# Sliding-window attention: value products and spreads issued two units at a time, their outputs copied and scaled once per pair

## The chip, the cores and the metric

One core of one Trainium2 chip runs the whole program. The metric is the device time of one execution in microseconds (us), and the lower it is the better. The engines are TensorE (PE in the rows, its weight loads PEld), VectorE (DVE), ScalarE (ACT), GpSimd (POOL) and SyncE (SP, which here only issues DMAs). Each engine takes its own instructions in order, and semaphores join them.

## The reference, cut to what matters

The reference is two blocks of two layers on 512 tokens of width 1024. The change touches one stage of it, the sliding-window attention of the second block, and nothing else:

```
q = q.reshape(B, nb, BLOCK, N_KV_HEADS, Q_PER_KV, HEAD_DIM)
...
scores = einsum("bnqgrd,bnkgd->bngrqk", q, kb) * (HEAD_DIM ** -0.5)
scores = scores - slopes * dist, masked outside the window
m = maximum(max(scores), sink)
p = exp(scores - m)
probs = p / (sum(p) + exp(sink - m))
out = einsum("bngrqk,bnkgd->bnqgrd", probs, vb)
return out.reshape(B, S, Q_DIM) @ w_o + b_o
```

There are 16 query heads in 4 groups (one key and value head each) and 4 blocks of 128 tokens. A block attends to itself and to the block before it; the first block has only itself.

## The kernel before, in words

The stage is worked in 16 **units**, u = 0 to 15. Unit u is key head g = u // 4 and token block n = u % 4, with the four query heads of that group. A unit with n = 0 has one block of keys instead of two, so about half the work in transposes and products.

What each unit needs, and who does it:

- **Scores** (TensorE, `swa_scores`, L1092): 12 matmuls into PSUM banks 0 and 1 for even units, 2 and 3 for odd ones.
- **Largest score** (VectorE, `swa_max`, L2357): the sink column is written (L2364), then four fused instructions add the distance term and take the minimum of the negated scores (L2366).
- **Exponentials** (ScalarE, `swa_exp`, L1700): four activations with their row sums (L1707). VectorE inverts the sums (`swa_inverse`, L2376).
- **Transposes** (TensorE, `swa_transposes`, L1111; recorded at the helper's line L643): four into bank 4 for the previous block of keys, if there is one, then four into bank 5 for the unit's own block. Banks 4 and 5 exist once each, so the transposes of unit u wait until both halves of the unit before were copied out (L1115 and L1117).
- **Copies** of the transposed probabilities (`spt`, two buffers): ScalarE copies bank 4 (`swa_copy`, L1713), VectorE copies bank 5 (`swa_copy`, L2370, the row at L2374).
- **Products** with the values (TensorE, `swa_pv`, L1122; rows at L1132): eight matmuls, four if n = 0, into one half of bank 6.
- **Spread** of the inverted sums over the partitions (TensorE, `swa_spread`, L1138; rows at L1146): eight matmuls into one half of bank 7.
- **Output**: ScalarE copies the unit's half of bank 6 to `so` (`swa_out`, L1719), and VectorE multiplies it with the half of bank 7 (`swa_scaled`, L2381, row at L2386).

ScalarE's plain copies all have the line L1318. After each group of four units `so` is split in two parts: ScalarE's `swa_hi` (L1726) and VectorE's `swa_low` (L2389, row at L2392), which wait for the group's scalings. In units 10 to 13 VectorE also splits a quarter each of the first weight panel of the output projection (`split_piece`, L1855, rows at L1860 and L1861).

The order on each engine is written out by hand:

```
PE:  scores(0) scores(1); for u: scores(u+2), transposes(u), pv(u-1), spread(u-1);
     then spread(15), pv(15), output projection
ACT: exp(0); for u: exp(u+1), copy(u) if u % 4, out(u-1), at u = 5, 9, 13 hi
DVE: max(0), values of four token blocks, max(1); for u: inverse(u), max(u+2), copy(u),
     scaled(u-1), at u = 6, 10, 14 low, at u = 10 to 13 split_piece
```

The output projection (`out_projection`, L866) follows on TensorE. Its first panel is taken one tile of the contraction at a time, 6 matmuls each, and tile i waits for the i-th `swa_low` (semaphore "mixed"). Weight panels come by DMA from SyncE.

Of the kernel before, what the change touches and what calls it, by code (L numbers as in the profile page):

```python
# [34 lines left out]
P = 128  # L35
D = 1024
KT = D // P
TX, TC = 512, 256
# [52 lines left out]
def build_kernel(nc, dram, out):  # L91
    with ExitStack() as ctx:
# [44 lines left out]
        ps = ctx.enter_context(nc.psum_tensor("ps", [P, 8, 512], F32))  # L137
# [64 lines left out]
        so, sqh = place("so", 25600, [8, TX]), parts("sqh", 25600, [8, TX])  # L202
# [214 lines left out]
        def _(pe):  # L417
# [291 lines left out]
            for e in range(2, 16):  # L709
                if 4 <= e < 12:  # L710
                    side, j = ROPE[e - 4]
# [225 lines left out]
            for t in range(2):  # L937
                for f in range(4):
                    for c in range(2):
                        at = f % 2 * 256 + c * P  # L940
# [181 lines left out]
            def swa_pv(u):  # L1122
                g, n = u // 4, u % 4
                pe.wait_ge(sa["copied"], WITH_PREV[u + 1])
                pe.wait_ge(sa["copied_dve"], u + 1)
                if u:
                    pe.wait_ge(sa["out"], u)
                if u == 1:
                    pe.wait_ge(sa["v_prev"], 2)
                for kt in range(0 if n else 1, 2):  # L1130
                    for half in range(2):
                        last = pe.matmul(ps[64 * half:64 * half + 64, 6, u % 2 * 256:u % 2 * 256 + 256],  # L1132
                                         (sv if kt else svp)[:, n - 1 + kt, g * 64:g * 64 + 64],
                                         spt[u % 2][:, kt, half * 256:half * 256 + 256],
                                         start=kt == (0 if n else 1), stop=kt == 1)
                last.then_inc(sa["pv"], 1)

            def swa_spread(u):  # L1138
                pe.wait_ge(sa["inverse"], u + 1)
                if u:  # L1140
                    pe.wait_ge(sa["scaled"], u)
                for j in range(2):
                    for half in range(2):
                        at = 32 + 4 * (u % 4) + 2 * half + j
                        to = u % 2 * 256 + j * P
                        last = pe.matmul(ps[64 * half:64 * half + 64, 7, to:to + P],  # L1146
                                         stat[:, at:at + 1].broadcast_to([P, 64]), ident, start=True, stop=True)
                last.then_inc(sa["spread"], 1)
# [3 lines left out]
            for u in range(16):  # L1152
                if u + 2 < 16:
                    swa_scores(u + 2)
                if u == 0:
                    pe.wait_ge(v_free, 4)
                swa_transposes(u)
                if u:
                    swa_pv(u - 1)
                    swa_spread(u - 1)  # L1160
            swa_spread(15)
            swa_pv(15)
            out_projection("wo", "mixpost0", h2hi, h2lo, sa["mixed"])
# [138 lines left out]
        def _(act):  # L1302
# [14 lines left out]
            def copy(o, in_, func=ACT.Identity, **kw):  # L1317
                return act.activation(o, in_, func, **kw)  # L1318
# [231 lines left out]
            for k in range(4):  # L1550
                n, s = FIRST["out0"] + k, k % 2
# [164 lines left out]
                    act.wait_ge(sa["pv"], u - 1)  # L1716
                copy(spt[u % 2][:, 0, :], ps[:, 4, :]).then_inc(sa["copied"], 1)

            def swa_out(u):  # L1719

                g, n = u // 4, u % 4
                act.wait_ge(sa["pv"], u + 1)
                copy(so[:, 2 * g:2 * g + 2, n * P:(n + 1) * P],
                     ps[:, 6, u % 2 * 256:u % 2 * 256 + 256].rearrange("p (j n) -> p j n", j=2)).then_inc(sa["out"], 1)

            def swa_hi(g):  # L1726
                act.wait_ge(sa["scaled"], 4 * (g + 1))
                for t in range(2 * g, 2 * g + 2):
                    copy(h2hi[:, t, :], so[:, t, :]).then_inc(sa["mixed_hi"], 1)

            swa_exp(0)
            for u in range(16):
                if u + 1 < 16:
                    swa_exp(u + 1)
                if u % 4:
                    swa_copy(u)
                if u:
                    swa_out(u - 1)
                if u % 4 == 1 and u > 4:
                    swa_hi(u // 4 - 1)  # L1740
            swa_out(15)
            swa_hi(3)
            out_copy("wo", "mixpost0", ywo, "b_o")

# [86 lines left out]
        def _(dve):  # L1831
# [315 lines left out]
            for u, (hp, t, a) in enumerate(EVEN_UNITS):  # L2147
                n = TA if t < 4 else TC
# [5 lines left out]
                p = prob[u % 3]  # L2154
# [223 lines left out]
                dve.wait_ge(sa["exp"], 4 * (u + 1))  # L2378
                dve.reciprocal(stat[:, 32 + o:36 + o], stat[:, 16 + o:20 + o]).then_inc(sa["inverse"], 1)

            def swa_scaled(u):  # L2381
                g, n = u // 4, u % 4
                o = so[:, 2 * g:2 * g + 2, n * P:(n + 1) * P]
                dve.wait_ge(sa["out"], u + 1)
                dve.wait_ge(sa["spread"], u + 1)
                dve.tensor_tensor(o, o, ps[:, 7, u % 2 * 256:u % 2 * 256 + 256].rearrange("p (j n) -> p j n", j=2), ALU.mult)\  # L2386
                    .then_inc(sa["scaled"], 1)

            def swa_low(g):  # L2389
# [12 lines left out]
            for u in range(16):  # L2402
                swa_inverse(u)
                if u + 2 < 16:
                    swa_max(u + 2)
                swa_copy(u)
                if u:
                    swa_scaled(u - 1)
                if u % 4 == 2 and u > 4:
                    swa_low(u // 4 - 1)  # L2410
                if 10 <= u < 14:
                    split_piece(FIRST["wo"], u - 10)
            swa_scaled(15)
            swa_low(3)
            split_at(FIRST["wo"] + 1)
            out_splits("wo", "mixpost0")
# [107 lines left out]
            for t in range(4):  # L2524
# [5 lines left out]
                o = final[:, t, :]  # L2530
                step(dve.scalar_tensor_tensor(out=o, in0=ps[:, 2 * t:2 * t + 2, :].rearrange("p b n -> p (b n)"),
                                              scalar=stat[:, 8 + t:9 + t], in1=gpost[:, :], op0=ALU.mult, op1=ALU.mult))
                at = 0
# [192 lines left out]
```

## Time and profile before

| | |
|---|---|
| median of 3 runs | 2267.95 us (2266.7 to 2269.53) |
| span of the profiled execution | 2264.1 us |
| sliding-attention stage, first scores to first matmul of the output projection | 980.05 to 1040.10 us of the span |
| mean granted clock of TensorE over the span | 0.983 |

The profiled execution is given by its span, from its first to its last instruction; its own device time is not listed apart. The span is 3.9 us under the median of the runs. A granted clock of 1.00 is 2.4 GHz, 0.50 is 1.2 GHz. In a timeline a row gives the start in us from the span's start, the duration, the engine, the line and the instruction, how many followed each other (x8), and in brackets the idle time before it with the instruction that ended it. Consecutive instructions of one engine overlap in these records, so the cost of one in a row of others is the distance from its start to the next start, which is shorter than its duration.

### The profile page before, as it was taken

Reading aid. Unit: us, or ns where it says so; the run is one execution under the profiler, and the core shown is the slowest. Engines: PE = TensorE matmul, PEld = TensorE weight load, DVE = VectorE, ACT = ScalarE, POOL = GpSimd, SP = SyncE. Lnnn points to the kernel's source line nnn. Section 1 sums busy time; section 2 is a strip of 40 time slices with the busy share of each in tenths; the row PEclk is TensorE's granted clock in tenths of the full one; section 3 lists DMA queues with packets and bytes.
Section 4 is the critical chain, followed back from the end, with each engine's and each line's share of the span. In section 5 each row is a group of like instructions: output and inputs, shape, how many; then the busy total and the mean of one; then the engine's idle time right before and its main releaser. Section 6 shows DMA issues by size and latency. Waiting matters only on the chain.

```text
span 2264.1 us, 28233 instructions
## 1 busy us (share of the span) xinstructions
PE 2183.2 (96%) x11848; PEld 1778.1 (79%) x11848; DVE 1352.5 (60%) x1763; ACT 558.9 (25%) x1088; POOL 47.2 (2%) x31
## 2 busy tenths in 40 slices
PE   8999997899999999999999999999999999999998
PEld 5788885568788667777788888788888887888887
DVE  5123548884561474766697763454788536977733
ACT  4110007862320462364311110121101002211100
POOL 0000000000000020300000000000000000000000
PEclk9999998999899999999999999999999999999999
DMA  7332222312132021202222222222222222222321
GB/s 315 118 112 112 112 69 53 85 57 94 56 106 73 21 73 60 90 2 81 87 93 93 93 84 101 94 93 93 94 75 79 92 94 90 93 93 95 115 97 75
DMA packets 34238, 204.52 MB, mean 90 GB/s; under 512 B 4800, under 2 KB 5056, under 8 KB 14656
## 3 DMA queue, kind: packets, MB, share of 16 engines
q1 hardware_dynamic: 32736, 197.99, 25.0%
q10 hardware_dynamic: 1376, 4.72, 0.6%
q8 instruction: 94, 1.54, 0.3%
q14 instruction: 32, 0.26, 0.0%
HBM read 191.16 MB, written 2.10 MB: 85 GB/s over the span
## 4 chain that ended last, share of the span: by engine, by line
PE 88%; DVE 8%; ACT 3%; issue 1%; DMA 0%; DVEq 0%; SPq 0%; ACTq 0%
PE ps L422 23%; PE ps L423 22%; PE ps L424 22%; PE ps L528 3%; PE ps L530 3%; PE ps L529 3%; PE ps L643 2%; DVE stat L2128 2%; PE ps L577 1%; PE ps L982 1%; PE ps L1277 1%; PE ps L560 1%; PE ps L749 1%; PE ps L624 1%; ACT prob L1483 1%
## 5 line engine op out<-in xcount | busy, mean ns | idle before, releaser
L1851 DVE CAST whi<-raw 128x2048 fp32r<-128x2048 f32 (+2 forms) x148 | 172.0, 1162 | 430.9 <-DMA raw<-in_ffn_out 106.0
L422 PE MATMUL ps<-h2hi,whi 128*128 128x512 f32 (+1 forms) x1052 | 412.2, 392 | 4.6 <-DVE h2lo L1951 4.4
L424 PE MATMUL ps<-h2hi,wlo 128*128 128x512 f32 (+1 forms) x1052 | 407.2, 387 | 0.0
L423 PE MATMUL ps<-h2lo,whi 128*128 128x512 f32 (+1 forms) x1052 | 406.9, 387 | 0.0
L1852 DVE TENSOR_TENSOR wlo<-raw,whi 128x2048 fp32r<-128x2048 f32 (+2 forms) x148 | 320.1, 2163 | 5.1
L422 PE MATMUL ps<-h1hi,whi 128*128 128x512 f32 (+1 forms) x768 | 272.3, 354 | 3.4 <-DVE h1lo L2037 1.4
L423 PE MATMUL ps<-h1lo,whi 128*128 128x512 f32 (+1 forms) x768 | 268.7, 350 | 0.0
L424 PE MATMUL ps<-h1hi,wlo 128*128 128x512 f32 (+1 forms) x768 | 266.5, 347 | 0.0
L422 PEld LDWEIGHTS ps<-h2hi,whi 128*128 128x128 f32 x1052 | 197.6, 188 | 51.2 <-DVE h2lo L1951 9.9
L424 PEld LDWEIGHTS ps<-h2hi,wlo 128*128 128x128 f32 x1052 | 197.5, 188 | 40.7
L423 PEld LDWEIGHTS ps<-h2lo,whi 128*128 128x128 f32 x1052 | 197.7, 188 | 38.7
L422 PEld LDWEIGHTS ps<-h1hi,whi 128*128 128x128 f32 x768 | 146.5, 191 | 27.3 <-issue 3.6
L423 PEld LDWEIGHTS ps<-h1lo,whi 128*128 128x128 f32 x768 | 146.2, 190 | 19.3 <-issue 1.4
L424 PEld LDWEIGHTS ps<-h1hi,wlo 128*128 128x128 f32 x768 | 145.9, 190 | 19.6
L422 PE MATMUL ps<-mhi,whi 128*128 128x512 f32 x368 | 143.5, 390 | 0.0
L424 PE MATMUL ps<-mhi,wlo 128*128 128x512 f32 x368 | 143.2, 389 | 0.0
L423 PE MATMUL ps<-mlo,whi 128*128 128x512 f32 x368 | 143.2, 389 | 0.0
L2436 DVE TENSOR_TENSOR temp<-ps,rxs 128x1024 f32<-128x1024 f32 x44 | 53.9, 1225 | 80.9 <-PE ps L424 78.4
L1318 ACT ACTIVATE temp<-ps 128x512 f32<-128x512 f32 (+1 forms) x41 | 21.3, 555 | 314.2 <-PE ps L424 298.5
L1318 ACT ACTIVATE tap<-temp,pc 128x512 f32<-128x512 f32 x44 | 36.1, 820 | 244.0 <-DVE temp L2436 244.0
L424 PEld LDWEIGHTS ps<-mhi,wlo 128*128 128x128 f32 x368 | 69.1, 188 | 14.5
L422 PEld LDWEIGHTS ps<-mhi,whi 128*128 128x128 f32 x368 | 69.1, 188 | 14.3
(325 smaller groups left out, 3339.5 us busy)
## 6 DMA issues: line engine op xcount, KB each, us to landing
raw<-in_ffn_in SPq DMA_DIRECT2D x44, 1024.0 KB, 4.9
raw<-in_even SPq DMA_DIRECT2D x16, 1024.0 KB, 7.1
mod_w<-in_mod SPq DMA_DIRECT2D x6, 2048.0 KB, 19.2
raw<-in_odd SPq DMA_DIRECT2D x12, 1024.0 KB, 4.9
raw<-in_sgu_v SPq DMA_DIRECT2D x12, 1024.0 KB, 4.8
raw<-in_sgu_u SPq DMA_DIRECT2D x12, 1024.0 KB, 4.8
raw<-in_sgu_out SPq DMA_DIRECT2D x16, 768.0 KB, 4.3
raw<-in_ffn_out SPq DMA_DIRECT2D x16, 704.0 KB, 4.0
```

The lines of the kernel that those rows point to most:

```text
L422: pe.matmul(o, r(lhi), r(rhi), start=first, stop=False, **kw)
L423: pe.matmul(o, r(lhi), r(rlo), start=False, stop=False, **kw)
L424: return pe.matmul(o, r(llo), r(rhi), start=False, stop=last, **kw)
L528: pe.matmul(o, lhi, rhi, start=kt == 0, stop=False)
L529: pe.matmul(o, lhi, rlo, start=False, stop=False)
L530: return pe.matmul(o, llo, rhi, start=False, stop=kt == KT - 1)
L643: return pe.transpose(o, in_, ident)
L1318: return act.activation(o, in_, func, **kw)
L1851: step(dve.tensor_copy(whi[:, slot, 0:width].bitcast(F32R), raw[:, slot, 0:width]))
L1852: tell(dve.tensor_tensor(wlo[:, slot, 0:width].bitcast(F32R), raw[:, slot, 0:width], whi[:, slot, 0:width], ALU.subtract), split_done, n + 1)
L2128: dve.tensor_reduce(stat[:, o:o + 2], scr, AX, ALU.max, negate=True).then_inc(ea["negmax"], 1)
L2436: tell(dve.tensor_tensor(gu[s], ps[:, b:b + 2, :], rxs[:].unsqueeze(1).broadcast_to([P, 2, TX]), ALU.mult), ff["scaled"], c0 + n + 1)
```

## The change

Products and spreads of units u-2 and u-1 are issued together, behind the transposes of every second unit, u = 2, 4, ... 14. The order there is both products, then both spreads. Behind the transposes of odd units nothing is left, and the loop goes on with the next scores. After the loop come spread(14), pv(14), spread(15), pv(15). ScalarE copies bank 6 once per pair, and VectorE multiplies with bank 7 once per pair; both instructions are 128x512 instead of 128x256, and stand at even u. The waits on "out" and "scaled" count pairs. The number of TensorE's instructions stays; ScalarE and VectorE have 8 fewer each. Nothing about DMAs changes.

```diff
--- before.py
+++ after.py
@@ -1123,8 +1123,8 @@
                 g, n = u // 4, u % 4
                 pe.wait_ge(sa["copied"], WITH_PREV[u + 1])
                 pe.wait_ge(sa["copied_dve"], u + 1)
-                if u:
-                    pe.wait_ge(sa["out"], u)
+                if u % 2 == 0 and u:
+                    pe.wait_ge(sa["out"], u // 2)
                 if u == 1:
                     pe.wait_ge(sa["v_prev"], 2)
                 for kt in range(0 if n else 1, 2):
@@ -1137,8 +1137,8 @@
 
             def swa_spread(u):
                 pe.wait_ge(sa["inverse"], u + 1)
-                if u:
-                    pe.wait_ge(sa["scaled"], u)
+                if u % 2 == 0 and u:
+                    pe.wait_ge(sa["scaled"], u // 2)
                 for j in range(2):
                     for half in range(2):
                         at = 32 + 4 * (u % 4) + 2 * half + j
@@ -1155,9 +1155,13 @@
                 if u == 0:
                     pe.wait_ge(v_free, 4)
                 swa_transposes(u)
-                if u:
-                    swa_pv(u - 1)
-                    swa_spread(u - 1)
+                if u and u % 2 == 0:
+                    for v in (u - 2, u - 1):
+                        swa_pv(v)
+                    for v in (u - 2, u - 1):
+                        swa_spread(v)
+            swa_spread(14)
+            swa_pv(14)
             swa_spread(15)
             swa_pv(15)
             out_projection("wo", "mixpost0", h2hi, h2lo, sa["mixed"])
@@ -1716,15 +1720,15 @@
                     act.wait_ge(sa["pv"], u - 1)
                 copy(spt[u % 2][:, 0, :], ps[:, 4, :]).then_inc(sa["copied"], 1)
 
-            def swa_out(u):
-
-                g, n = u // 4, u % 4
-                act.wait_ge(sa["pv"], u + 1)
-                copy(so[:, 2 * g:2 * g + 2, n * P:(n + 1) * P],
-                     ps[:, 6, u % 2 * 256:u % 2 * 256 + 256].rearrange("p (j n) -> p j n", j=2)).then_inc(sa["out"], 1)
+            def swa_out(v):
+
+                g, at = v // 2, v % 2 * TC
+                act.wait_ge(sa["pv"], 2 * v + 2)
+                copy(so[:, 2 * g:2 * g + 2, at:at + TC].rearrange("p j (u n) -> p u j n", u=2),
+                     ps[:, 6, :].rearrange("p (u j n) -> p u j n", u=2, j=2)).then_inc(sa["out"], 1)
 
             def swa_hi(g):
-                act.wait_ge(sa["scaled"], 4 * (g + 1))
+                act.wait_ge(sa["scaled"], 2 * (g + 1))
                 for t in range(2 * g, 2 * g + 2):
                     copy(h2hi[:, t, :], so[:, t, :]).then_inc(sa["mixed_hi"], 1)
 
@@ -1734,11 +1738,11 @@
                     swa_exp(u + 1)
                 if u % 4:
                     swa_copy(u)
-                if u:
-                    swa_out(u - 1)
+                if u and u % 2 == 0:
+                    swa_out(u // 2 - 1)
                 if u % 4 == 1 and u > 4:
                     swa_hi(u // 4 - 1)
-            swa_out(15)
+            swa_out(7)
             swa_hi(3)
             out_copy("wo", "mixpost0", ywo, "b_o")
 
@@ -2378,12 +2382,12 @@
                 dve.wait_ge(sa["exp"], 4 * (u + 1))
                 dve.reciprocal(stat[:, 32 + o:36 + o], stat[:, 16 + o:20 + o]).then_inc(sa["inverse"], 1)
 
-            def swa_scaled(u):
-                g, n = u // 4, u % 4
-                o = so[:, 2 * g:2 * g + 2, n * P:(n + 1) * P]
-                dve.wait_ge(sa["out"], u + 1)
-                dve.wait_ge(sa["spread"], u + 1)
-                dve.tensor_tensor(o, o, ps[:, 7, u % 2 * 256:u % 2 * 256 + 256].rearrange("p (j n) -> p j n", j=2), ALU.mult)\
+            def swa_scaled(v):
+                g, at = v // 2, v % 2 * TC
+                o = so[:, 2 * g:2 * g + 2, at:at + TC].rearrange("p j (u n) -> p u j n", u=2)
+                dve.wait_ge(sa["out"], v + 1)
+                dve.wait_ge(sa["spread"], 2 * v + 2)
+                dve.tensor_tensor(o, o, ps[:, 7, :].rearrange("p (u j n) -> p u j n", u=2, j=2), ALU.mult)\
                     .then_inc(sa["scaled"], 1)
 
             def swa_low(g):
@@ -2404,13 +2408,13 @@
                 if u + 2 < 16:
                     swa_max(u + 2)
                 swa_copy(u)
-                if u:
-                    swa_scaled(u - 1)
+                if u and u % 2 == 0:
+                    swa_scaled(u // 2 - 1)
                 if u % 4 == 2 and u > 4:
                     swa_low(u // 4 - 1)
                 if 10 <= u < 14:
                     split_piece(FIRST["wo"], u - 10)
-            swa_scaled(15)
+            swa_scaled(7)
             swa_low(3)
             split_at(FIRST["wo"] + 1)
             out_splits("wo", "mixpost0")
```

## Rows read from the trace of the kernel before

**Rows 1.** The page's list of busy time by engine, whole span
```profile
PE 2183.2 (96%) x11848; PEld 1778.1 (79%) x11848; DVE 1352.5 (60%) x1763; ACT 558.9 (25%) x1088; POOL 47.2 (2%) x31
```

**Rows 2.** Windows: stretch; length, busy us (count) of PE, PEld, DVE, ACT, POOL; clock; DMA
```profile
992.00:1040.00 48.00, 43.93 (x466) 33.17 (x462) 41.89 (x164) 36.05 (x133) 0.00 (x0) 1.00 0.13 45
```

**Rows 3.** Source view of the transposes, waits of TensorE: releaser, us in total, times
```profile
  DVE spt L2374: 5.6, 6
```

**Rows 4.** Timeline of PE: start, us, line, tiles, shapes, count, idle before
```profile
1000.98 0.39 PE L1107 MATMUL ps<-whi,sqh 64*128 64x256 f32 x2
...
1001.88 1.09 PE L643 MATMUL ps<-mats,sprob 128*128 128x128 f32 x8
1002.90 0.65 PE L1132 MATMUL ps<-spt,sv 128*64 128x256 f32 x4
...
1025.76 0.63 PE L643 MATMUL ps<-mats,sprob 128*128 128x128 f32 x4 [1.39 <-DVE spt L2374]
1026.31 0.65 PE L1132 MATMUL ps<-spt,svp 128*64 128x256 f32 x4
...
1027.23 0.61 PE L1146 MATMUL ps<-mats,stat 128*64 128x128 f32 x8
```

**Rows 5.** Timeline of DVE, same columns, two stretches of the stage
```profile
1001.99 0.17 DVE L2364 COPY ps<-stat 128x4 f32<-128x4 f32 x1 [0.16 <-PE ps L1107]
...
1003.67 0.69 DVE L2374 COPY spt<-ps 128x512 f32<-128x512 f32 x1
1004.28 0.41 DVE L2386 TENSOR_TENSOR so<-so,ps 128x256 f32<-128x256 f32 x1
...
1020.79 1.28 DVE L2392 TENSOR_TENSOR h2lo<-so,h2hi 128x512 fp32r<-128x512 f32 x2
1022.00 0.42 DVE L1860 CAST whi<-raw 128x512 fp32r<-128x512 f32 x1
...
1023.18 0.18 DVE L2379 RECIPROCAL stat<-stat 128x4 f32<-128x4 f32 x1
...
1024.92 0.69 DVE L2374 COPY spt<-ps 128x512 f32<-128x512 f32 x1
```

**Rows 6.** Groups of ScalarE in the stage: busy us, mean ns, idle before
```profile
L1318 ACT ACTIVATE so<-ps 128x256 f32<-128x256 f32 x16 | 6.2, 389 | 11.0 <-PE ps L1132 11.0
```

**Rows 7.** Timeline of PE, first products, spreads and transposes of unit 2
```profile
990.35 0.65 PE L1132 MATMUL ps<-spt,sv 128*64 128x256 f32 x4
990.83 0.61 PE L1146 MATMUL ps<-mats,stat 128*64 128x128 f32 x8
991.37 0.33 PE L1107 MATMUL ps<-whi,sqh 64*128 64x128 f32 x2
...
992.18 1.09 PE L643 MATMUL ps<-mats,sprob 128*128 128x128 f32 x8
```

**Rows 8.** Timeline of DVE, the first scaling
```profile
991.55 0.42 DVE L2386 TENSOR_TENSOR so<-so,ps 128x256 f32<-128x256 f32 x1 [0.41 <-PE ps L1146]
```

**Rows 9.** Timeline of PE, spread and products of unit 15, then projection
```profile
1038.65 0.66 PE L1146 MATMUL ps<-mats,stat 128*64 128x128 f32 x8 [0.69 <-DVE so L2386]
1039.10 0.63 PE L1132 MATMUL ps<-spt,svp 128*64 128x256 f32 x4
...
1040.10 0.50 PE L422 MATMUL ps<-h2hi,whi 128*128 128x512 f32 x1
```

**Rows 10.** Timeline of PE, a restart behind a wait of 2.21 us
```profile
29.22 1.07 PE L560 MATMUL ps<-mod_w,cs 128*32 128x256 f32 x16 [2.21 <-ACT rows L1318]
```

**Rows 11.** Timeline of PE, the restart ahead of the stage's slow stretch
```profile
983.42 0.58 PE L1107 MATMUL ps<-whi,sqh 64*128 64x256 f32 x2 [1.73 <-ACT sprob L1707]
```

**Rows 12.** Windows, columns as in rows 2: two slow stretches, one with a wait
```profile
31.00:35.00 4.00, 4.00 (x15) 3.43 (x15) 3.59 (x9) 1.13 (x2) 0.00 (x0) 0.57 1.01 422
982.00:991.00 9.00, 6.81 (x44) 5.50 (x46) 8.41 (x39) 5.73 (x25) 1.55 (x2) 0.62 0.01 3
1031.00:1035.00 4.00, 2.40 (x24) 1.59 (x22) 3.93 (x16) 3.55 (x12) 0.00 (x0) 1.00 1.00 424
```

## The prediction

> **What bounds it now.** The page comes first [rows 1]: TensorE is busy for 96% of the span, so the question for the stage is which wait stops TensorE and what lies behind it. The windows table of the stage's settled part [rows 2] shows no engine with much room: in 48.00 us TensorE has 43.93 us of work and VectorE 41.89 us, at a clock of 1.00, and ScalarE 36.05 us. The source view of the transposes [rows 3] names the wait: VectorE's copy of bank 5, 6 times, 5.6 us in all. The timelines show when. Where VectorE has only unit work, TensorE goes on without a gap; where VectorE also has a split piece or the low parts, TensorE stands, once for 1.39 us [rows 4]. VectorE is thus the second bound, hidden only as far as it runs ahead of TensorE. What matters for this change is whether it still can.
>
> **What the change removes.** No matmul goes. On VectorE two multiplies of 0.41 us become one of 128x512. The trace has no such multiply, but it has a 128x512 copy out of PSUM on the same engine, whose next instruction starts 0.61 us after it [rows 5]; two of the old ones take 0.66 us at most, if one is a duration of 0.41 us less an overlap of 0.08 us, as that copy's (0.69 against 0.61). I take 0.61 us, the lower end, so the saving is 0.05 us a pair and up to nothing at the upper end. On ScalarE eight copies go at 389 ns a pair at most [rows 6]; that engine already waits 11.0 us for products in this very instruction, so I cost its side at nothing. If that cover went, the merged copy would cost at most 0.39 us more before the last scaling.
>
> The row of the copy and the row of the multiply (0.69 us for 512 columns, 0.41 us for 256) say that one large instruction saves 0.13 us of duration. The Trainium skill, page "VectorE: DVE Perf Modes", section on the TRN2 errata, states the same direction: a fixed cost is paid once per instruction, so a single large tile is better. By that rule the sum would be about 1 us shorter over 8 pairs (8 x 0.13 us); the trace agrees on the size, but it is worth that only where VectorE's work and not its place in the order is what counts.
>
> **What it moves.** The multiply of pair (u-2, u-1) stands in VectorE's queue behind copy(u) and waits for the last spread of the pair. Behind it wait the low parts, the split piece, inverse(u+1), max(u+3) and copy(u+1). And transposes(u+2) wait for copy(u+1). Before, each multiply waited for products and a spread that were short and one at a time; now TensorE puts four blocks ahead of it. This closes a loop of fixed length from the second half of transposes(u) to that of transposes(u+2), for even u:
>
> - second half of the transposes 0.55 us, from 1025.76 to 1026.31 [rows 4];
> - two products, 0.92 us each [rows 4], 0.48 us for a unit with n = 0 [rows 7]: 1.84 us, or 1.40 us if one of the two has n = 0;
> - two spreads, 0.54 us each [rows 7]: 1.08 us;
> - from the end of the spread to the multiply 0.18 us (0.72 us from 990.83 to 991.55, less 0.54) [rows 7, 8], and the multiply 0.61 us;
> - low parts 1.21 us (1020.79 to 1022.00) where u = 6, 10; a piece 1.18 us (1022.00 to 1023.18) where u = 10, 12; from inverse to copy 1.74 us (1023.18 to 1024.92) [rows 5];
> - from the start of the copy to the transposes 0.84 us (1024.92 to 1025.76) [rows 4, 5].
>
> Where nothing extra stands in the loop, max(u+3) waits for its scores instead: 1.01 us from their start to VectorE's start (1000.98 to 1001.99) and 1.68 us more to the copy [rows 4, 5], 2.69 us against 0.18 + 0.61 + 1.74 = 2.53 us. The loops are then
>
> u = 2: 0.55 + 1.40 + 1.08 + 2.69 + 0.84 = 6.56; u = 4: the same with 1.84, 7.00; u = 6: 0.55 + 1.40 + 1.08 + (2.53 + 1.21) + 0.84 = 7.61; u = 8: 7.00; u = 10: as u = 6 with a piece, 8.79; u = 12: 0.55 + 1.84 + 1.08 + (2.53 + 1.18) + 0.84 = 8.02. Together 44.98 us.
>
> The pieces of u = 11 and 13 cost 0.1 us at most: from copy(11) on, VectorE has 0.61 + 1.18 + 1.74 + 0.61 = 4.14 us of work until it is ready for the multiply, and TensorE's blocks let it begin after 0.84 + 3.03 + 0.18 = 4.05 us. TensorE's own work between two such points is shorter than the loop: for u = 4, 0.55 + 1.84 + 1.08 and two scores at 0.90, 1.02 and 0.51 of transposes, 6.80 us against 7.00. So TensorE waits at every even unit, least there, most at u = 12.
>
> Behind the last such point TensorE runs through: 0.55 + 1.40 + 1.08, transposes(15) 1.02 [rows 4], then spread, products, spread of 0.54 + 0.92 + 0.54 and the last products 1.00 us (1039.10 to 1040.10) [rows 9]: 7.05 us. The 0.69 us that the spread of unit 15 now waits for the multiply of unit 14 [rows 9] are gone in this sum. The multiply and the split behind the end are covered: tile 6 of the projection is read 36 matmuls later, over 8 us at 0.23 us each, and the last low part is late by some 0.5 us only.
>
> **The sum.** Before: the second half of transposes(2) starts half of 1.02 us after 992.18 [rows 7], at 992.69, and the projection at 1040.10 [rows 9], 47.41 us. After: 44.98 + 7.05 = 52.03 us, 4.62 us more. At the head unit 0's product and spread, 0.48 + 0.54 = 1.02 us, no longer stand before scores(4) and transposes(2) [rows 7], so the point comes 1.02 us earlier: +3.60 us. Like blocks in a row may also follow more closely. Bounds: nothing, or 0.15 us at each of the 7 double spreads (the eight of a block start 0.05 us apart, 0.39 us, and a block holds 0.54). The nearest row is the spread that is followed by products, 0.45 us (1038.65 to 1039.10) [rows 9], 0.09 us less than 0.54, so I take 7 x 0.09 = 0.63 us. That leaves +3.0 us, between +2.6 and +3.9 with the bounds of the multiply.
>
> **The clock.** The loops leave TensorE idle for about 1.8 us ahead of unit 8, 2.9 us ahead of unit 12 and 2.1 us ahead of unit 14 (a loop less TensorE's own blocks in it: 7.61 - 5.85, 8.79 - 5.85, 8.02 - 5.90). In this trace idle times of 2.21 and 1.73 us ended in a fall from the upper level (2.4 GHz) to the lower (1.2 GHz), at once in the second case [rows 10 to 12]: a mean of 0.57 over 4 us is 3.4 us at the lower level, a mean of 0.62 over 9 us is 6.8 us. A wait of about 1.6 us in the stage itself left 1.00 [rows 12], and so did that of 1.39 us [rows 4]. An idle time of 2.9 us is longer than all of them, so I count one fall, behind the wait of unit 12. Its price: 3.0 us of the loop are TensorE's (0.55 + 1.40 + 1.08). If 3.4 us at half speed begin at the restart they cost 1.7 us; if they begin 1.9 us later, as behind the idle time that ended at 29.22 (31 to 35 us in the table), 1.1 us of the loop are left and the cost is 1.1 us. I take 1.4 us, with bounds of 0 and 1.7 us. The sum is +3.0 + 1.4 = +4.4 us.
>
> The Trainium skill, page "TensorE: Matmul & The Clock Gate", Part 1, says that the slow level is the default and that activity releases it. The trace agrees with the two levels. Page "Perfetto Trace Analysis", section "Matmul Optimizations", advises matmuls back to back in batches for that reason; by it the grouped order would keep the clock and the sum would be +3.0 us. That is the first rival below, and the trace's 1.00 in the stage now leaves such a rule nothing to win.
>
> **How this stands to the runs.** The sum is of differences within one execution of 2264.1 us span; the median of the runs is 3.95 us above that, and I add the difference to the median: 2267.95 + 4.4 = 2272.3 us.
>
> **Rivals.**
> - No fall of the clock: +3.0 us, 2270.9 us. For it: waits of 1.4 and 1.6 us in the stage were harmless. Against: none of 2.9 us was. Chance 0.22.
> - Two or three falls, also ahead of units 8 and 14 (slower than before beyond what can be told): the idle time of 1.73 us that did end in a fall is as long as these. It decides from the second fall on, each again 1.4 us: +5.8 to +7.2 us, 2273.8 to 2275.2 us. Chance 0.22.
> - The loop does not close, because ScalarE's and VectorE's copies come in time as now. Then the head, the 0.69 us at the tail and the closer blocks are all that is left, -0.7 - 0.6 = -1.3 us, 2266.7 us; the head's 1.0 us only moves work. For it: VectorE has 6 us of room in 48 [rows 2]. Against: the multiply's wait for four blocks uses up that room in each pair. Chance 0.12.
> - The merged multiply or copy with its four-level pattern is dearer than the copy I took it from, by up to 0.2 us in each of 6 loops: +1.2 us on top, 2273.5 us. Chance 0.06.
>
> The forecast, one fall, has 0.38.
>
> **How the numbers follow.** What a measurement of this kernel can tell from no change is about 0.2%, 4.5 us, that is 2263.4 to 2272.5 us. The forecast lies just inside. Slower beyond it are the falls of the second rival (0.22, of which 0.2), the dearer multiply (0.05) and some two fifths of the forecast's own spread (0.16): 0.41. Faster beyond it would need more than every saving named, 0.03. The rest, 0.56, is within. The range goes from the case without a fall less its bounds and the 1.3 us by which runs differ, 2269.0 us, to three falls, 2275.4 us; the case without a loop is what stays out.
>
> **What would show it.** In the changed profile VectorE's multiply, 8 of them near 0.69 us, idles on the spreads nearly every time; TensorE idles ahead of the second half of transposes 4, 8, 12 and 14 on the copy of L2374, together 7 to 8 us against 5.6 us now; the stage from 980.05 us ends near 1044.5 us. A granted clock under 1.00 between 1028 and 1036 us is the fall. Wrong would be: no wait of the transposes of unit 12 over 2 us, or a stage that ends by 1041 us.

## The result: 0.25% slower, and the profile after

| | before | after |
|---|---|---|
| median of 12 runs each | 2268.93 us | 2274.97 us |
| ratio after to before | | 1.0025 (95% interval 1.0017 to 1.0034) |
| span of the profiled execution | 2264.1 us | 2266.4 us |
| stage, first scores to first matmul of the projection | 60.05 us | 63.91 us (978.38 to 1042.29) |
| second half of transposes(2) to the projection | 47.41 us | 52.22 us |

The change costs 5.7 us by the ratio (3.9 to 7.7 us). That is clear of no change, and its middle lies beyond the 4.5 us that the prediction took as the least that can be told; the lower end of the interval does not. The stage in the profiled execution is 3.86 us longer. The profiled run of the change, 2268.17 us, was the shortest of its twelve. Of everything else, the part behind the projection's first matmul takes 1224.0 us before and 1224.1 us after. The part ahead of the stage, whose instructions are the same, was 1.7 us shorter in this one execution; over all twelve profiles of this study it ran from 978.2 to 990.0 us with no order by kernel. So single spans say little here, and what follows compares the stage.

The page after and three windows (columns as in rows 2) of the stage, of the long wait in it and of the 4 us behind that wait:

```profile
span 2266.4 us, 28200 instructions
...
PE 2185.5 (96%) x11848; PEld 1780.3 (79%) x11848; DVE 1353.1 (60%) x1755; ACT 556.7 (25%) x1080; POOL 47.6 (2%) x31
```

```profile
978.38:1042.29 63.91, 54.16 (x546) 41.60 (x545) 51.63 (x201) 42.43 (x154) 1.55 (x2) 0.92 0.09 34
1023.00:1026.00 3.00, 0.23 (x4) 0.03 (x2) 2.97 (x13) 1.33 (x6) 0.00 (x0) 1.00 0.00 0
1026.00:1030.00 4.00, 3.93 (x20) 2.29 (x22) 3.50 (x13) 0.60 (x4) 0.00 (x0) 0.57 0.02 4
```

VectorE and TensorE have the same work as before: VectorE is busy for 51.63 us of the stage against 51.84 us, and TensorE has 11848 matmuls in the whole span both times. The clock is new: 0.57 behind a wait, where the stage of the kernel before had 1.00 from 992 us on [rows 2]. The source view of the transposes (TensorE's waits: releaser, us, times), which answers to [rows 3]:

```profile
  DVE spt L2378: 8.9, 7
```

8.9 us against 5.6 us. The view counts waits of the matmuls and of their weight loads. The source view of VectorE's multiply, its form and its own waits:

```profile
L2390 DVE TENSOR_TENSOR so<-so,ps x8: 686/686/689, 993.1 to 1043.0; 128x512 f32<-128x512 f32 x8
...
  PE ps L1146: 7.9, 7
```

All eight are 0.69 us long, and seven of them wait for a spread, 7.9 us in total; the last one, behind the end of the stage, waits 1.9 us for ScalarE's copy. Now TensorE's timeline; transposes with a wait are the second halves of units 4, 8, 12 and 14:

```profile
989.56 1.09 PE L643 MATMUL ps<-mats,sprob 128*128 128x128 f32 x8
...
996.44 0.63 PE L643 MATMUL ps<-mats,sprob 128*128 128x128 f32 x4 [0.63 <-DVE spt L2378]
...
1005.12 1.04 PE L1146 MATMUL ps<-mats,stat 128*64 128x128 f32 x16
...
1010.66 0.63 PE L643 MATMUL ps<-mats,sprob 128*128 128x128 f32 x4 [1.66 <-DVE spt L2378]
1011.22 0.65 PE L1132 MATMUL ps<-spt,svp 128*64 128x256 f32 x4
...
1013.00 1.04 PE L1146 MATMUL ps<-mats,stat 128*64 128x128 f32 x16
1013.97 0.39 PE L1107 MATMUL ps<-whi,sqh 64*128 64x256 f32 x2
...
1026.07 0.78 PE L643 MATMUL ps<-mats,sprob 128*128 128x128 f32 x4 [2.84 <-DVE spt L2378]
1026.78 1.12 PE L1132 MATMUL ps<-spt,svp 128*64 128x256 f32 x4
...
1035.48 0.66 PE L643 MATMUL ps<-mats,sprob 128*128 128x128 f32 x4 [1.49 <-DVE spt L2378]
...
1042.29 0.50 PE L422 MATMUL ps<-h2hi,whi 128*128 128x512 f32 x1
```

and VectorE's timeline of the loop from unit 6 to unit 8:

```profile
1006.28 0.69 DVE L2390 TENSOR_TENSOR so<-so,ps 128x512 f32<-128x512 f32 x1 [1.05 <-PE ps L1146]
1006.88 1.28 DVE L2396 TENSOR_TENSOR h2lo<-so,h2hi 128x512 fp32r<-128x512 f32 x2
1008.09 0.17 DVE L2383 RECIPROCAL stat<-stat 128x4 f32<-128x4 f32 x1
...
1009.83 0.69 DVE L2378 COPY spt<-ps 128x512 f32<-128x512 f32 x1
```

Read the two together as one chain. The sixteen spread matmuls start at 1005.12 and fill 0.97 us. The multiply starts 0.19 us behind them (1006.28), then come the low parts, the inverse at 1008.09, the four maxima, the copy at 1009.83, and 0.83 us later the transposes of unit 8 (1010.66), for which TensorE has stood 1.66 us. Nothing in the chain waits for anything outside it.

### The profile page after: what moved, and what is told of

It reads as the page before. It is cut to its first block, busy times and chain, and to the rows that moved or that the text cites. A ratio compares the mean times of both kernels' runs of the same rounds, so it can differ in the third digit from the quotient of the medians.

```text
span 2266.4 us, 28200 instructions
## 1 busy us (share of the span) xinstructions
PE 2185.5 (96%) x11848; PEld 1780.3 (79%) x11848; DVE 1353.1 (60%) x1755; ACT 556.7 (25%) x1080; POOL 47.6 (2%) x31
## 3 DMA queue, kind: packets, MB, share of 16 engines
q8 instruction: 94, 1.54, 0.3%
## 4 chain that ended last, share of the span: by engine, by line
PE 88%; DVE 8%; ACT 2%; issue 1%; DMA 0%; DVEq 0%; SPq 0%; ACTq 0%
PE ps L422 23%; PE ps L423 22%; PE ps L424 22%; PE ps L528 3%; PE ps L529 3%; PE ps L530 3%; PE ps L643 2%; DVE stat L2132 2%; PE ps L577 1%; PE ps L1281 1%; PE ps L560 1%; PE ps L982 1%; PE ps L749 1%; PE ps L1132 1%; PE ps L624 1%
## 5 line engine op out<-in xcount | busy, mean ns | idle before, releaser
L423 PEld LDWEIGHTS ps<-mlo,whi 128*128 128x128 f32 x368 | 69.1, 188 | 14.4
```

What stands on the lines that cost most here:

```text
L423: pe.matmul(o, r(lhi), r(rlo), start=False, stop=False, **kw)
```

## The experiments

Ten kernels ran, two of them (the change and e6) twice. The stage is read from the first scores to the first matmul of the projection, and its settled part from the start of transposes(2). This table has every one of them:

```
kernel                                ratio (interval)          stage   transposes(2) on  waits of units 8, 12, 14
before                                                          60.05   47.92             0.20 1.39  1.60
the change                            1.0025 (1.0017, 1.0034)   63.91   52.73             1.66 2.84  1.49
the change again, e8                  1.0040 (1.0026, 1.0054)   64.05   52.74             1.66 2.85  1.49
e1 merged outputs, old order          1.0008 (0.9993, 1.0023)   60.95   47.49             0.34 1.52  1.86
e2 new order, outputs not merged      1.0022 (1.0010, 1.0034)   65.70   54.64             1.73 2.91  1.54
e3 the change, multiply later         1.0004 (0.9991, 1.0017)   61.73   50.59             0.19 0.29  1.29
e4 the change, pieces at odd units    1.0001 (0.9989, 1.0013)   60.27   48.90             1.66 1.66  0.48
e5 the change, long wait filled       1.0009 (0.9997, 1.0021)   62.14   51.03             1.66 (full) 1.49
e6 e1 and pieces at odd units         0.9997 (0.9986, 1.0009)   57.58   45.09             0.33 0.33  0.68
e10 the same again                    0.9975 (0.9964, 0.9986)   57.22   45.11             0.34 0.34  0.67
e7 before, pieces at odd units        1.0004 (0.9992, 1.0016)   58.21   45.94             0.19 0.18  0.41
e9 e6 and the stage's start filled    0.9958 (0.9944, 0.9973)   55.69   45.11             0.34 0.34  0.68
```

The ratios are each against runs of before on the same chip. The last column has TensorE's waits for VectorE's copy of the unit before; waits for ScalarE are not in it.

### The two halves of the change: e1 and e2

e1 undoes TensorE's order and keeps the merged copy and multiply:

```diff
-                if u and u % 2 == 0:
-                    for v in (u - 2, u - 1):
-                        swa_pv(v)
-                    for v in (u - 2, u - 1):
-                        swa_spread(v)
-            swa_spread(14)
-            swa_pv(14)
+                if u:
+                    swa_pv(u - 1)
+                    swa_spread(u - 1)
             swa_spread(15)
```

> TensorE has the order of before (products and spread of one unit behind every unit's transposes); ScalarE's copy and VectorE's multiply are merged per pair as in the change. Theory (the place of the double block in front of the multiply closes a loop through VectorE's queue): only one product and one spread stand ahead of the multiply, so it is ready 1.4 to 1.5 us earlier, VectorE does not fall behind, and the stage from the first scores to the first matmul of the projection takes 59.5 us, at most the 60.05 us of before; TensorE's wait ahead of the transposes of unit 12 is about 1.5 us, not 2.8. Rival (the merged instructions are what costs): the stage keeps most of the change's 63.6 us. Time against before: the theory expects 0.9995, the rival 1.0020 or more.

TensorE's waits ahead of the transposes of units 12 and 14 in its timeline:

```profile
1028.62 0.63 PE L643 MATMUL ps<-mats,sprob 128*128 128x128 f32 x4 [1.52 <-DVE spt L2374]
...
1036.18 0.65 PE L643 MATMUL ps<-mats,sprob 128*128 128x128 f32 x4 [1.86 <-DVE spt L2374]
```

1.52 us at unit 12, as expected. The settled part takes 47.49 us, 0.43 us less than before. The whole stage takes 60.95 us, over the 59.5 expected, because its first 13.5 us, ahead of transposes(2), are 1.3 us longer than before. In this execution the slow stretch at the stage's start came later: the clock is 0.97 in the first 6.8 us and 0.52 in the 6.65 us behind them. The time is not told from no change (1.0008, up to 1.0023). In the settled part, merging the outputs costs nothing.

e2 is the other half: the order of the change, with two copies and two multiplies of 128x256 at every second unit:

```diff
-                if u:
-                    swa_scaled(u - 1)
+                if u and u % 2 == 0:
+                    swa_scaled(u - 2)
+                    swa_scaled(u - 1)
...
-                dve.wait_ge(sa["spread"], u + 1)
+                dve.wait_ge(sa["spread"], u // 2 * 2 + 2)
```

(ScalarE's copies likewise, and TensorE's order and waits as in the change.)

> TensorE has the order of the change (two products, two spreads behind every second unit); ScalarE copies and VectorE multiplies each unit by itself, 128x256, both behind the pair's last product and spread. Theory: the loop is the same and 0.05 us longer, so TensorE waits ahead of the second half of transposes 4, 8, 12 and 14 as in the change (0.6, 1.7, 2.9, 1.5 us) and the stage takes 62 us without a fall of the clock and 63.7 us with one. Rival (the merged instructions cost): near the 60.05 us of before. Time against before: the theory expects 1.0015 to 1.0030, the rival 1.0000.

Its waits ahead of transposes 12 and 14, and the clock in the 4 us behind the first and 3 us behind the second:

```profile
1037.70 1.09 PE L643 MATMUL ps<-mats,sprob 128*128 128x128 f32 x4 [2.91 <-DVE spt L2380]
...
1047.15 0.65 PE L643 MATMUL ps<-mats,sprob 128*128 128x128 f32 x4 [1.54 <-DVE spt L2380]
```

```profile
1037.00:1041.00 4.00, 3.30 (x16) 2.03 (x18) 3.67 (x15) 1.23 (x6) 0.00 (x0) 0.58 0.01 4
1049.00:1052.00 3.00, 3.00 (x26) 2.28 (x23) 0.60 (x2) 1.08 (x3) 0.00 (x0) 0.61 0.41 172
```

All four waits of the change are there, each 0.05 to 0.07 us longer at units 8, 12 and 14. The loss is in TensorE's order. This execution had two slow stretches, so its stage is 1.8 us longer still, about 0.2 us of it from the longer waits. The second one came behind a wait of 1.54 us; behind the 1.49 us at the same place in the change and in e8 below none came.

### Where the multiply stands: e3

```diff
-                if u and u % 2 == 0:
+                if u > 2 and u % 2 and u < 15 or u == 14:
                     swa_scaled(u // 2 - 1)
```

> The change, with VectorE's multiply of a pair moved behind max and copy of the next odd unit (the last two pairs as in the change). Theory: the copy of the odd unit no longer waits for the spreads, so TensorE's waits ahead of the transposes of units 8 and 12 go from 1.7 and 2.8 us to about 0.3 us each, and VectorE's idle time on spreads goes from 7.9 us to under 3 us; the pieces and the low parts then weigh on the last units, where about 1.5 us of wait for the copy and 1 us for ScalarE's stay, so the stage takes 61.5 to 62 us. No wait is over 2 us, so no fall of the clock between units 10 and 15. Rival (TensorE's own double blocks cost, wherever the multiply stands): waits and stage as in the change, 63.6 us.

TensorE's waits ahead of the transposes of units 8 and 12:

```profile
1015.57 0.63 PE L643 MATMUL ps<-mats,sprob 128*128 128x128 f32 x4 [0.19 <-DVE spt L2378]
...
1029.56 0.63 PE L643 MATMUL ps<-mats,sprob 128*128 128x128 f32 x4 [0.29 <-DVE spt L2378]
```

The waits view of the stage (who waited for whom, us in total, times, longest):

```profile
ACT h2hi L1322 <- DVE so L2390: 6.3, 3, 2.6
...
PE ps L1107 <- ACT sprob L1711: 4.6, 6, 1.7
...
PEld ps L1107 <- ACT sprob L1711: 6.2, 6, 1.9
...
PE ps L643 <- DVE spt L2378: 2.4, 4, 1.3
```

TensorE's waits for the copy ahead of units 8 and 12 shrink from 1.66 and 2.84 us to 0.19 and 0.29 us, the spreads hold VectorE no more, and the clock stays 1.00 from transposes(2) on. The stage takes 61.73 us, as expected. What it still loses is a new wait: ScalarE's high parts now wait for the later multiply, 6.3 us in total, the exponentials stand behind them in its queue, and the scores of later units wait for these (0.62 and 0.37 us at units 9 and 10, and again at 13 and 14); unit 15's transposes wait 1.19 us for a copy of ScalarE. So the place in the queue set the waits of the change, but moving the instruction moves most of the loss to the next one that depends on it: the settled part is 2.14 us shorter than in the change, and 1.70 us of that is the price of the clock alone, as e5 below shows.

### Where the pieces stand: e4

```diff
-                if 10 <= u < 14:
-                    split_piece(FIRST["wo"], u - 10)
+                if u >= 9 and u % 2:
+                    split_piece(FIRST["wo"], (u - 9) // 2)
```

> The change, with the four split pieces of the first projection panel at units 9, 11, 13 and 15 instead of 10 to 13. Theory: behind the copy of an odd unit VectorE waits for TensorE's four blocks anyway, so a piece there is hidden, while one at an even unit lengthens the loop by its whole 1.18 us. The waits ahead of the transposes of units 12 and 14 shrink by 1.2 and 1.0 us to 1.7 and 0.7 us, and the stage takes 2.2 us less, 60.4 us, or 3.8 us less than the profiled 63.6 us if the fall of the clock behind the longer wait goes too. Rival (VectorE's sum of work counts, not its place): no change against the 63.6 us.

The remaining waits at units 12 and 14:

```profile
1030.88 0.63 PE L643 MATMUL ps<-mats,sprob 128*128 128x128 f32 x4 [1.66 <-DVE spt L2378]
...
1037.64 0.66 PE L643 MATMUL ps<-mats,sprob 128*128 128x128 f32 x4 [0.48 <-DVE spt L2378]
```

The same work on VectorE, moved by one or two units, takes the wait of unit 12 down by 1.18 us, exactly one piece, and that of unit 14 by 1.01 us. Without the 2.84 us wait there is no slow stretch. The stage takes 60.27 us, 3.64 us less than with the change, and the ratio returns to 1.0001. VectorE's sum of work is the same, so the rival falls. The change is not cured by this: the kernel before with its pieces at the same places (e7) has a stage of 58.21 us, 2.06 us less.

### The price of the clock: e5 and e8

```diff
                     elif u:
+                        if u == 12:
+                            pe.wait_ge(sa["scaled"], 5)
+                            for _ in range(3):
+                                pe.matmul(ps[:, 7, :], ident, mats.rearrange("p m n -> p (m n)"), start=True, stop=True)
                         pe.wait_ge(sa["copied_dve"], u)
```

> The change, with three idle-time matmuls of 128x512 (fp32, into bank 7, whose contents are consumed) ahead of the second half of transposes(12), where TensorE waits 2.8 us for VectorE's copy. They take about 0.85 us each and end before the copy does, so the order and the wait's end stay. Theory (a fall of the clock follows the long idle time and is a price of its own): the granted clock stays 1.00 between transposes 12 and 14, that loop takes 8.0 us instead of the 9.4 us profiled for the change, and the stretch from transposes(2) to the projection 51.2 to 51.4 us instead of 52.7 us; a fall behind the 1.5 us wait of unit 14 may still come. Rival (the loop of unit 12 is longer for another reason, VectorE or ScalarE): still 9.4 us with a clock of 1.00.

TensorE's timeline of the filled wait and of the next one (L1120 are the added matmuls, whose result nobody reads):

```profile
1022.89 2.84 PE L1120 MATMUL ps<-mats 128*128 128x512 f32 x6
1025.72 0.66 PE L643 MATMUL ps<-mats,sprob 128*128 128x128 f32 x4
1026.30 0.65 PE L1136 MATMUL ps<-spt,svp 128*64 128x256 f32 x4
...
1033.51 0.66 PE L643 MATMUL ps<-mats,sprob 128*128 128x128 f32 x4 [1.49 <-DVE spt L2382]
```

The row counts each added matmul twice, so one takes 0.94 us, not 0.85 us. They fill the wait and do not prolong it: the transposes of unit 12 start at 1025.72, 2.83 us behind the first of them. But the products behind it take 0.65 us for four instead of 1.12 us, and from here to the second half of transposes(14) it is 7.79 us instead of 9.41 us. The slow stretch cost 1.62 us of this loop, and the stage takes 62.14 us, 1.77 us less. The rest of the change's loss, 2.09 us against before, is the loop at full clock.

> The change once more, on the chip of the filled wait. Theory: the same waits ahead of transposes 4, 8, 12 and 14 (0.6, 1.7, 2.8, 1.5 us) as in its first profile, since they are given by the loop; what can differ is the clock, whose falls come behind the waits of 2.8 and 1.5 us in one or two places. Stretch from transposes(2) to the projection 51.3 us without, 52.7 us with one, 54.5 us with two falls. Time against before 1.0015 to 1.0035. If instead the waits themselves vary by more than 0.2 us between executions, the loop is not the cause of them.

The same kernel as the change, once more: its waits repeat to 0.01 us and its stage to 0.14 us. They belong to the order, not to the execution. The time came out at 1.0040 of before, above the 1.0015 to 1.0035 that was expected.

### What beats both kernels: e6, e7, e10 and e9

e6 puts together e1 and the pieces of e4, e7 is before with the pieces alone, and e10 is e6 again.

> TensorE in the order of before, outputs merged per pair, split pieces at units 9, 11, 13 and 15. Behind an odd unit's copy VectorE has no multiply and has room. The theory gives a stretch from transposes(2) to the projection of 45.3 us against 47.9 us before and 47.5 us with the merge alone: waits ahead of transposes 12 and 14 of 0.4 and 0.9 us instead of 1.5 and 1.9 us. Time against before 0.9988. Rival (VectorE's total of work in the stage is the bound, wherever it stands): 47.5 us as with the merge alone.

> The kernel before with only the split pieces moved to units 9, 11, 13 and 15. It tells what of the gain of the version with merged outputs is due to the pieces alone. Expected: 46.0 us from transposes(2) to the projection against 47.9 us before, of which 0.7 us is still the wait of the spread of unit 15; time against before 0.9992. If the merge matters as much as the place of the pieces, this is slower than the merged version by 0.7 us or more in the profile.

> The version with TensorE's old order, merged outputs and the pieces at odd units once more, unfilled, to stand beside the filled one on one chip. Stage 57.6 us as in its first profile, 45.1 us from transposes(2) to the projection; time against before 0.9988. The first measurement, 0.9997 with an interval of 0.9986 to 1.0009, did not tell it from no change; together they should show whether 2.5 us of stage reach the time.

Windows from transposes(2) to the projection (columns as in rows 2), first e7, then e6:

```profile
995.25:1041.19 45.94, 43.90 (x463) 33.08 (x461) 41.56 (x163) 35.50 (x133) 0.00 (x0) 1.00 0.13 47
```

```profile
997.06:1042.15 45.09, 43.73 (x462) 33.05 (x460) 40.84 (x156) 33.79 (x120) 0.00 (x0) 1.00 0.13 48
```

45.94 us with the pieces alone and 45.09 us with the merge too, against 47.92 us: the place of the pieces is worth 1.98 us and the merge 0.85 us more. That the spread of unit 15 no longer waits 0.68 us for the multiply of unit 14 is most of the second. In time, e6 was not told from before (0.9997) and e10 was (0.9975), with the same kernel and the same settled part; the two intervals only touch, at 0.9986, so how much of 2.5 to 2.8 us of stage reaches the time stays rough. e7's time (1.0004) is not told from before either. The expected lengths of these stages held within 0.4 us, the expected times (0.9988 to 0.9992) less well.

e9 adds to this version what e5 did, at the stage's start, where all kernels here wait 1.72 to 1.73 us for the first exponentials and then run slowly:

```diff
             for u in range(16):
+                if u < 2:
+                    for _ in range(2):
+                        pe.matmul(ps[:, 7, :], ident, mats.rearrange("p m n -> p (m n)"), start=True, stop=True)
                 if u + 2 < 16:
                     swa_scores(u + 2)
```

> The version with TensorE's old order, merged outputs and the pieces at odd units, plus two matmuls of 128x512 (fp32, 0.85 us each at 2.4 GHz, into bank 7, result unused) ahead of scores(2) and of scores(3), where TensorE waits 1.72 and up to 1.9 us for the first exponentials in all kernels here. Theory (the slow stretch behind these waits costs time of its own): the clock stays 1.00 through the stage's start, the stretch from the first scores to transposes(2) takes 10.6 us instead of 12.1 to 12.5 us, the rest stays at 45.1 us, and the stage takes 55.7 us against 57.6 us unfilled and 60.05 us before. Time against before 0.9980. Rival (the start is bound by VectorE's and ScalarE's chain, whatever the clock): 12.1 us or more for the first stretch, stage 57.5 us.

Windows of the stage's first part and of the rest, first e10, then e9:

```profile
986.09:998.20 12.11, 9.61 (x86) 7.89 (x85) 9.60 (x45) 8.13 (x34) 1.55 (x2) 0.72 0.01 2
998.20:1043.31 45.11, 43.75 (x463) 33.06 (x461) 40.86 (x156) 33.82 (x120) 0.00 (x0) 1.00 0.13 48
```

```profile
984.11:994.69 10.58, 10.54 (x93) 7.04 (x93) 9.32 (x45) 7.69 (x33) 1.55 (x2) 1.00 0.01 2
994.69:1039.80 45.11, 43.74 (x462) 33.06 (x460) 40.86 (x156) 34.11 (x122) 0.00 (x0) 1.00 0.13 48
```

The clock goes from 0.72 to 1.00, the first part from 12.11 to 10.58 us, the rest stays at 45.11 us, and the stage takes 55.69 us. The kernel takes 0.9958 of before's time, the fastest of the study. It was expected at 0.9980, outside the interval: the 9.5 us that the ratio stands for (from six runs) are more than the 4.4 us by which its stage is shorter. On the same chip e10 has 5.7 us in time for 2.8 us of stage.

## Why the prediction was right or wrong

**Time and sign.** The median, 2274.97 us, is inside the range, 2.7 us above the forecast and only 0.4 us under the range's top; 1.0 us of the 2.7 us is that the median of before was 2268.93 us over twelve runs and 2267.95 us over the three I had. The change is slower by more than the 4.5 us that I had set, to which I had given 0.41 against 0.56 for within. By the stage alone it would have been as forecast: +3.86 and +4.00 us in two profiles against +4.4 us. That it comes this close is in part luck: the loops and the tail were forecast 0.9 us too long and the fall of the clock 0.2 to 0.4 us too cheap. The time itself lies where the rival of two or three falls stood (2273.8 to 2275.2 us), while both profiles of the change show one.

**The loop.** Right, and the main thing. It was to run from the transposes over two products, two spreads, multiply, extras, maxima and copy back to the transposes:

```
loop from the second half of transposes(u), us    u=2   u=4   u=6   u=8   u=10  u=12
forecast                                          6.56  7.00  7.61  7.00  8.79  8.02
measured in the change                            6.37  6.77  7.45  6.78  8.63  9.41 (7.79 in e5)
```

(A second half of transposes without a wait has no row of its own. For units 6 and 10 its start is taken 0.56 us before the products, as in the rows with a wait; for unit 2, which does not wait, half of 1.02 us behind the first half, at 990.07.) At full clock every loop came out 0.16 to 0.23 us shorter, 1.2 us in all. Two of my terms were too long: the double spread takes 0.97 us, 0.11 us less than 1.08 (I had taken 0.09 us off in the sum), and two full products take 1.78 us (1011.22 to 1013.00), not 1.84. The rest are hundredths in the waits. So the sum without the clock was +2.97 us, and e5 measured +2.09 us; of the difference 0.56 us are the loops, less the 0.63 us counted there already, 0.24 us is the run behind unit 14, below, and 0.07 us is that the filled wait of unit 12 ended a little earlier in e5: together 0.87 of the 0.88 us.

**Costed at nothing.** ScalarE's merged copy hid, as e1 shows, whose settled part is shorter than before with it. The pieces of units 11 and 13 hid too. Behind the piece of unit 11 VectorE's multiply starts 0.19 us behind the spreads at full clock (e5, 1029.05 to 1029.24), which is the time it takes without a piece; the one new wait there, 0.34 us at unit 14, is for ScalarE's copy and ends ahead of the longer one for VectorE's. e4 shows that a piece counts whole at an even unit.

**The merged multiply.** 0.69 us each, as taken from the copy. The rival of a dearer pattern falls. The fixed cost that the Trainium skill states (page "VectorE: DVE Perf Modes", section on the TRN2 errata) is there in the durations, 0.69 us for one of 512 columns against 2 x 0.41 us for two of 256, and it did not decide: e2 pays it 8 times more and its waits grow by 0.05 to 0.07 us a loop.

**The clock.** One fall at the wait of unit 12 was forecast, and it came in all three profiles with an idle time near 2.9 us there, the change, e8 and e2; in e5, e4 and e3, where TensorE was not idle for that long, it did not come. I took 1.4 us for it, e5 gives 1.6 to 1.8 us (1.62 us in the loop, 1.70 us from transposes(2) on, 1.77 us in the stage). The advice of the page "Perfetto Trace Analysis", section "Matmul Optimizations" of the Trainium skill, matmuls back to back in batches, did not help in this case: the settled part of the stage had a clock of 1.00 without the batches, and with them the idle time of 2.84 us behind which it fell.

**The head.** Transposes(2) start 11.18 us behind the first scores instead of 12.13 us, 0.95 us earlier against 1.02 us forecast. The tail: no wait of unit 15's spread, as forecast, and 6.81 us from transposes(14) to the projection against 7.05 us.

**The signs.** The waits ahead of the second half of transposes 4, 8, 12 and 14 are 6.6 us together in the timeline, under the 7 to 8 us that I named. The 5.6 us that I set against it is from the view that counts weight loads too, and that view has 8.9 us now. The stage set at 980.05 us would end at 1043.96 us against 1044.5 us. Two numbers of the prediction do not come out of its own terms: the median of before stands 3.85 us over the span, not 3.95 us, which enters no sum, and the range by its terms is 2269.2 to 2275.2 us, not 2269.0 to 2275.4 us; the measured median is in both.

**Open.** The ratio stands for 5.7 us and the stage for 3.9 us in its profiles; e8's ratio stands for 9 us with the same stage. The lower ends of the two intervals, 3.9 and 5.9 us, leave 0 to 2 us without a cause shown, their middles 1.8 and 5 us. The clocks of the runs say where to look. In the 81 runs of before that have one on record, a mean granted clock lower by 0.001 goes with about 1.1 us more time. On e8's chip the change has 0.9775 on average and before 0.9803. By that slope this is 3.1 us of the 7.2 us between their means, an estimate, and the 4.1 us that are left are close to the 4.0 us of the stage. One slow stretch as in the profile (0.57 over 4 us) lowers the mean of a whole run by only 0.0008; it is in both numbers, so up to 1 us stays open even then. The two profiled runs of the change have 0.980 and 0.981, above their means. So most runs of the change had more time at the lower clock than its profiles show. A second slow stretch as in e2 would add 1.8 us, but no profile says where in the program the rest lies. e9, with 0.9830 against 0.9788, has its surplus in the same way: 4.6 us by the slope, 4.8 us left for a stage that is 4.4 us shorter.

## What to carry to other kernels

Grouping work on the engine that seemed to be the bound did nothing for it here, and delayed the engine that consumes the group. Before doing the same, look at what stands in the consumer's queue behind the instruction that waits for the group, and whether that engine comes back to feed the first one. If so, add up the closed chain; if it is longer than the first engine's own work between the same two points, the difference is lost each time round. Work that fills in from elsewhere (here split pieces of a weight panel) cost its whole length in such a chain, 1.18 us a piece, and nothing beside it, so look at its place before its size.

## What the hardware showed that was not expected

TensorE's clock fell to 1.2 GHz at the stage's start in all eleven profiles without filling there, behind the idle time of 1.72 us ahead of scores(2) or the next one ahead of scores(3), and yet stayed at 2.4 GHz behind the 1.66 us wait of unit 8, the 1.49 us wait of unit 14 in the change, and even behind 1.86 us in e1. In e2 the 1.54 us wait of unit 14 was followed by a slow stretch. A length near 1.5 to 1.9 us alone does not tell it. Filling such a wait with matmuls whose result nobody reads, 2.84 us for three, kept 2.4 GHz both times it was tried (e5, e9). It delayed nothing in e5; in e9 scores(2) came 3.49 us behind the first scores instead of 3.36 us, and yet the stretch of 12.1 to 12.5 us (e10 and e6) became 10.58 us.
